# Context rows in the recurrence units: a ring of seven buffers in front of the wide ring, and a unit's 21 rows spread over its sixteen places

## The reference

```python
def peer(h, p, l):
    ...                                  # product keys: 8 heads x 16 experts of 16384 per token
    def chunk(args):
        xc, ic, gc = args
        act = jax.nn.gelu(jnp.einsum('cd,ced->ce', xc, u_tab[ic]), approximate=False) * gc
        return jnp.einsum('ce,ced->cd', act, v_tab[ic])
```

## Time and profile before

| | |
|---|---|
| median of 3 runs | 2637.39 us (2623.78 to 2640.93) |
| span of the profiled execution | 2634.3 us |
| TensorE busy | 2362.0 us (90%) |
| VectorE busy | 1772.4 us (67%) |
| GpSimd busy | 938.1 us (36%) |
| mean granted TensorE clock | 0.934 |

### The profile page before, as it was taken

One profiled execution on the slowest core, in us unless ns is written; L12 is line 12 of the kernel. 1 busy time (PEld: TensorE's weight loads), 2 busy tenths in 40 slices (PEclk: granted clock), 3 DMA queues, 4 the chain that ended last, 5 costly groups with the idle time before them and its releaser, 6 DMA issues.

```text
span 2634.3 us, 43615 instructions
## 1 busy us (share of the span) xinstructions
PE 2362.0 (90%) x18034; PEld 1656.0 (63%) x18034; DVE 1772.4 (67%) x3464; ACT 497.0 (19%) x1002; POOL 938.1 (36%) x774
## 2 busy tenths in 40 slices
PE   5998977888878887999889889999999999999997
PEld 2544545766767776334468777776776777775664
DVE  0111254335677785587689886789899888876767
ACT  2111123324334432100122211000000100000101
POOL 0000000000144443154441003766665666774653
PEclk8998987988989997999899869999999999999998
DMA  9233041130165665286896006999999999999997
GB/s 307 96 112 144 0 143 42 31 131 2 60 220 192 213 209 190 114 312 242 293 366 227 17 33 244 371 394 384 404 408 360 408 409 409 405 395 412 409 409 310
DMA packets 199455, 647.01 MB, mean 246 GB/s; under 512 B 25222, under 2 KB 27142, under 8 KB 198298
## 3 DMA queue, kind: packets, MB, share of 16 engines
q0 software_dynamic: 110592, 402.70, 40.5%
q1 hardware_dynamic: 88666, 241.52, 24.5%
HBM read 635.50 MB, written 8.65 MB: 245 GB/s over the span
## 4 chain that ended last, share of the span: by engine, by line
PE 54%; DVE 16%; DMA 15%; issue 7%; POOL 4%; ACT 4%; SPq 1%; DVEq 0%; POOLq 0%; ACTq 0%
DMA arena<-in_peer_v,arena 9%; PE ps L1078 8%; PE ps L1089 8%; PE ps L599 7%; PE ps L1100 5%; DMA arena<-in_peer_u,arena 5%; PE ps L1054 4%; POOL arena L2252 3%; PE ps L1004 2%; PE ps L1019 2%; DVE arena L2078 2%; PE ps L601 2%; PE ps L850 2%; DVE arena L1904 1%; POOL arena L2240 1%
## 5 line engine op out<-in xcount | busy, mean ns | idle before, releaser
L1089 PE MATMUL ps<-arena 128*128 128x512 f32 x1024 | 466.2, 598 | 20.5 <-DVE arena L2117 20.5
L1078 PE MATMUL ps<-arena 128*128 128x256 f32 x2048 | 478.4, 388 | 0.0
L2252 POOL DMA_INDIRECT arena<-in_peer_u,arena x256 | 341.1, 1333 | 341.2 <-DVE arena L1871 186.7
L1078 PEld LDWEIGHTS ps<-arena 128*128 128x128 f32 x2048 | 391.2, 194 | 68.6 <-issue 19.7
L2252 POOL DMA_INDIRECT arena<-in_peer_v,arena x256 | 299.9, 1171 | 202.5 <-DVE arena L2078 142.3
L2078 DVE SCALAR_TENSOR_TENSOR arena<-arena 128x1024 f32<-128x1024 f32 x252 | 315.6, 1282 | 81.3 <-DMA arena<-in_peer_v,arena 80.4
L2240 POOL DMA_INDIRECT arena<-in_peer_u,arena x128 | 152.9, 1195 | 576.8 <-DVE arena L1871 318.4
L1089 PEld LDWEIGHTS ps<-arena 128*128 128x128 f32 x1024 | 194.6, 192 | 219.7 <-issue 212.6
L2073 DVE SCALAR_TENSOR_TENSOR arena<-arena 128x1024 bf16<-128x1024 f32 x256 | 303.8, 1221 | 41.1 <-DMA arena<-in_peer_u,arena 40.1
L1100 PEld LDWEIGHTS ps<-arena 128*128 128x128 bf16 x3072 | 205.9, 156 | 69.6 <-issue 47.0
L1100 PE MATMUL ps<-arena 128*128 128x32 bf16 x3072 | 208.6, 243 | 23.3 <-DVE arena L2110 22.5
(11 more groups left out here) (361 smaller groups left out, 3340.7 us busy)
## 6 DMA issues: line engine op xcount, KB each, us to landing
arena<-in_uT SPq DMA_DIRECT2D x128, 512.0 KB, 6.8
arena<-in_peer_v SPq DMA_DIRECT2D x128, 512.0 KB, 6.8
arena<-in_w_ada SPq DMA_DIRECT2D x12, 2048.0 KB, 13.9
arena<-in_peer_wq SPq DMA_DIRECT2D x12, 2048.0 KB, 10.5
arena<-in_w_in SPq DMA_DIRECT2D x6, 2048.0 KB, 8.0
arena<-in_w_out SPq DMA_DIRECT2D x4, 2048.0 KB, 9.1
arena<-in_peer_u,arena POOLq DMA_INDIRECT x384, 11.1
arena<-in_peer_v,arena POOLq DMA_INDIRECT x384, 11.1
```

The source lines that it names most:

```text
L1078: m = pe.matmul(ps[:, 4 + i % 2, 0:ND], us[i % UB][:, k, :], hTd[:, k, :], start=(k == 0), stop=(k == KD - 1))
L1089: m = pe.matmul(ps[:, 2 * r + c, :], sgel[:, i % SBUFS, P * r:P * r + P], vs[i % VB][:, 512 * c:512 * c + 512], start=(i == 0), stop=(i == ...
L2252: pool.indirect_dma_start(gring[:, n % RING, :], None, a[("peer_u", "peer_v")[e]][0], bass.IndirectOffsetOnAxis(ap=ids[:, t, m:m + 1], axi ...
```

## The change

The first 126 context rows use a ring of seven buffers. The three new ones lie where the states of the recurrence and the context's r and k values lay (`sn`, `st2[0]`, the start of `rkv`), so GpSimd waits, before its first row, for the stores of the final states, for `sn_ok` and for the context's `gm_ok`. The wide ring of eight keeps its place; its four extra slots are numbered so that row 125 and row 132 share one. The wait for `gm_ok` at 5 moves from the fifth row of the wide ring (row 130) to its first (row 126). A unit takes 21 rows as before: two at places 0, 1, 4, 7 and 10, one at each other place, where it took four at place 0, three at place 1 and one elsewhere. SP waits for 125 used rows before it loads `g2` and `ftab`, which overwrite one of the new buffers.

```diff
-CR = 4
+CR, EXTRA = 4, 3
...
-        k = n % CR if n < WIDE_FROM else (n - WIDE_FROM) % slots if n < WIDE_TO else (n - WIDE_TO) % CR
+        k = n % (CR + EXTRA) if n < WIDE_FROM else (n - WIDE_FROM) % slots if n < WIDE_TO else (n - WIDE_TO) % CR
...
-UNIT_ROWS = {0: 4, 1: 3} | {l: 1 for l in range(2, 16)}
+UNIT_ROWS = {l: 2 if l in (0, 1, 4, 7, 10) else 1 for l in range(16)}
...
-        gring_c = [at(x.offset + i * D, D) for i in range(CR)] + [at(w_end + i * D, D) for i in range(CR)]
+        gring_c = [at(x.offset + i * D, D) for i in range(CR)] + [at(w_end + i * D, D) for i in (1, 2, 0, 3)]
+        gring_u = gring_c[0:CR] + [at(sn.offset, D), at(st2[0].offset, D), at(w_end, D)]
...
             sp.wait_ge(S("unit_ok"), len(UNITS))
+            sp.wait_ge(S("c_used"), WIDE_FROM - 1)
             sp.dma_start(g2, a["rwkv_g2"][0]).then_inc(S("ld_g2"), 16)
...
-                    slot, dst = gring_c[k], acc_c[c % 2]
+                    slot, dst = (gring_u if c < WIDE_FROM else gring_c)[k], acc_c[c % 2]
...
             pool.wait_ge(S("eid_ok"), 1)
+            pool.wait_ge(S("out_state"), 16 * 16)
+            pool.wait_ge(S("sn_ok"), 1)
+            pool.wait_ge(S("gm_ok"), 1)
...
-                elif k >= CR:
+                if n == WIDE_FROM:
                     pool.wait_ge(S("gm_ok"), NT)
-                pool.indirect_dma_start(gring_c[k], None, a[("peer_u", "peer_v")[e]][0],
+                pool.indirect_dma_start((gring_u if n < WIDE_FROM else gring_c)[k], None, a[("peer_u", "peer_v")[e]][0],
```

## The result

The changed kernel took **2588.93 us** (median of 4 runs, 2586.74 to 2591.70); the kernel before, on the same chip, took 2635.40 (4 runs). The ratio is **0.983, 95% interval 0.980 to 0.985**: faster by 1.7%. The prediction said 2581, range 2566 to 2610.

The account below looks back on a forecast made before the run. No engine bounds everywhere; in the last six units VectorE waits for gathered rows and TensorE for sigmoids. Gains 37.5 + 12.5 + 3.5 + 2.9 = 56.4 off 2634.3 give 2577.9; the median, 3.1 higher, gives 2581 us, range 2566 to 2610.

Parts of the forecast that it names:

- Where the wait was: Units 4 to 9: VectorE waits 49.9 us for gathered rows, TensorE 24.9 us for sigmoids; both waits would go.
- forecast gain of units 4 to 8: Five units, 272.5 us from first to last, would take 47.0 us each, 235.0 together: 37.5 us gained.
- the front of a unit: Places 0 and 1: four rows, 4.6 us, hide below the 6.8 us at which the sigmoid's VectorE step can start.
- The term for the refill wait: Middle of a unit: the eighth row in the burst waits 0 to 0.8 us for its slot; 0.8 taken.
- Clock: Units 4 to 8: with the sigmoid waits gone, TensorE's granted clock is unit 0's, 2.4 GHz throughout.
- over 0.97: Sign to check: the granted clock in units 4 to 8 is above 0.97.
- rival C: Clock stays low: units keep 2.5 us of slow matmuls, unit 9 gains 9.8, filters nothing; 2600 us, chance 0.15.
- Rival B: Burst starves: each GpSimd issue takes 1.99 + 0.30 us, units take 49.5 us; 2593 us, chance 0.17.
- Unit 9 and the filters: Last unit and filters behind it: shorter waits and full clock gain 12.5 us and 3.5 us (bounds 0 and 7).
- row waits of up to 3.8 us "covered": Unit 9: 20.6 us of VectorE work before a step due at 24.4 us behind M hides 3.8 us of waits.
- the prediction asked for 31: Sign to check: unit 9's L897 (now L899) starts within 31 us of M, the end of pairs 2 and 3's mask.
- Wide ring: Its start: rows 126 to 131 land early, part of the wait moves to row 132; 2.9 us gained.

Follow-up runs that it names:

- both edits: Changed kernel with place 15's row at place 2 and unit 9's rows waiting for TensorE's levels: 2631.57 us (0.992) on chip B, 2640.99 (0.997) on C.

## Why the prediction was right, and where it wasn't

*Where the wait was.* Right, on chip A. The waits for rows and for the sigmoids went, and with them nine tenths of the forecast gain of units 4 to 8 (34.3 of 37.5). The reason given was only half of it: the prediction let the new order do the work at the front of a unit, and the ring do it in the middle. The ring does both; the order alone moves the wait to L899.

*Middle of a unit.* The term for the refill wait was 0.8 us a unit and measured 0. L1952 came at 33.7, not 33.0, for another reason:

*Clock.* Taken as unit 0's. Unit 4 has it (1.00, 46.3 us). In units 5 to 8 (0.96, where the prediction asked for over 0.97) the clock falls behind the 1.9 us wait of L830. Windows just behind M of unit 5 in the changed kernel:

```profile
756.00:760.00 4.00, 2.38 (x63) 2.39 (x64) 4.00 (x9) 0.60 (x1) 1.21 (x2) 0.85 0.91 344
760.00:764.00 4.00, 4.00 (x60) 4.00 (x59) 2.14 (x4) 0.89 (x2) 3.39 (x3) 0.72 0.67 184
```

L1640 is 1.6 us late by it, and four such units are 6.4 us less gain. It is half of what rival C has for the units. The wait alone doesn't make the clock fall. In the kernel with the ring only, on chip A, L830 waits 1.90 us at M of units 5 to 8 alike; the clock falls behind it in units 6 and 7 and stays at 1.00 in units 5 and 8. Without rows the wait is 1.5 to 1.7 us and the clock stays at 1.00; in the one-operand kernel on chip B a wait of 2.34 us at M of unit 6 is followed by no fall either. What decides is open. The edit that shortens the wait was only run where the clock didn't fall.

*Long issues.* Rival B's price was not paid in time, though its premise was met: in the burst of eight, issues of 1.99 us follow each other at 2.29, one for two rows, and the median of all issues in the units rose from 0.94 to 1.17 us. The burst didn't starve because seven rows were there when it began and it is eight long. What the prediction missed is the other form: in unit 9 one issue takes as long as the whole run of rows. It stood in its own rows, as the 3979 ns of the earlier trace rows.

*Unit 9 and the filters.* Forecast 12.5 and 3.5, measured 8.2 and -1.1. Both terms failed at the same step, row waits of up to 3.8 us "covered": the long issue made row waits of 4.14, 2.27 and 0.93 us, L1952 came at 29.0 us behind M rather than 24.4, L899 waited 2.00 us, started 32.7 us behind M (the prediction asked for 31) and the clock fell. With the rows of unit 9 spread the two stretches measure 11.7 and 5.6 against the kernel before.

*Wide ring.* Right: 3.2 for 2.9. Row 127 has no wait; VectorE waits at row 132, 5.98 us:

```profile
1067.32 1.28 DVE L1910 SCALAR_TENSOR_TENSOR arena<-arena 128x1024 f32<-128x1024 f32 x1 [5.98 <-DMA arena<-in_peer_v,arena]
```

*Later.* Nothing was given back behind L1006 (1470.9 and 1471.1). The terms measure 44.6 us in place of 56.4; the 4.7 us up to unit 4 came on top, so that the miss of 12 us shows as 7 to 8 in the total. They are no part of the change (5.2 us of gain lie ahead of M of unit 0, which the change doesn't touch): that much of the hit is luck.

*What had no term at all.* The prediction took one chip's trace for the kernel's. On chip B the gain was 0 and not 1.7%, and 2652 lies far outside its range, because TensorE stopped in units 3 to 9 for something that the first trace doesn't show. That this is its instruction stream, delayed behind the gathers on the DMA engines, is a guess. For it: the gaps stand mostly in the 64x64 matmuls, where most instructions go by in a microsecond, at a DMA share of 0.9, and not without rows. Against it: the semaphores of matmuls that had started, and by the trace ended, came up to 5.6 us late as well, which instructions that arrive late don't explain by themselves. The runs show only that the rows cause the stops and the chip matters. They don't show the path, nor why chip A with a share of 0.93 in unit 9 has none.

## What to carry to other kernels

When rows stand in front of a step that is waited for, ask first whether they are there in time; on chip A a deeper ring made the order of the rows almost indifferent, while the order without the ring only moved the wait. Look at the longest issue in a trace and not only at the median: it can grow with the change. Leave gaps in a run of two-operand VectorE instructions when GpSimd must issue gathers beside them: on chip A this alone gave back 10 us, and the version with gaps (0.980 on chip A, and with the row of place 15 moved 0.992 and 0.997 on B and C) is the better kernel. A gain that comes from crowding transfers beside dense small matmuls should be measured on more than one chip.

## What the runs showed of the hardware

- An issue of an indirect DMA on GpSimd takes 0.94 us alone, often 1.99 beside VectorE's rows, 3.98 beside four rows and 7.41 beside seven rows back to back in unit 9; with the one-operand instruction in the rows it is 0.94 each time.
- The granted clock stayed at the lower level through 14.0 us of L949 that followed a fall (0.91 in unit 9's window), and stayed at the upper through the same work where it hadn't fallen (3.70 us for each half).
- The changed kernel has TensorE gaps without a visible releaser on chip B (36 in five units, 12.8 us) and none on chip A; with both edits there are 28 on B and 31 on C. Without rows the units take 45.94 us on A and on C.
- On chip B the semaphores of TensorE's matmuls come late beside gathers (2.1 to 2.8 us at L890 in units 4 to 8, 5.6 us at L820 in unit 3), on chip A 0.02 to 0.03 us behind the matmul's end.
- The clock fell behind a TensorE wait of 1.90 us in two units and not in two others of the same execution.
